# Order and shape of side work in a two-block transformer kernel on one TensorE: weights rounded ahead of the last evacuation, gate products with a 16-column stationary operand, squares and delta rule reordered

## The reference, cut to what matters

```
up = dwconv3(h @ w_in); gate, val = split(up)          # both MLPs, F = 5632
m  = (silu(gate) * val) @ w_out
x  = x + rmsnorm(m, norm_post_ffn)                     # first block: norm of the product
x  = x + m                                             # second block
gb, ga = the last 16 columns of h @ w_in_2             # 8 heads each
beta = sigmoid(gb)
g    = -exp(a_log) * softplus(ga + dt_bias);  g_cum = cumsum(g)  # per chunk of 64
q, k = l2norm(silu(conv4(q))) * 128 ** -0.5, l2norm(silu(conv4(k)))
lmat = where(strict, (k * beta) @ k.T * decay, 0);  t_inv = inv(eye + lmat)
attn = where(lower, q @ k.T * decay, 0)
out  = rmsnorm(delta_rule(q, k, v, beta, g), norm_g) * silu(z)
```

## Time and profile before

| | |
|---|---|
| median of three runs | 2841.45 us (2841.38 to 2842.84) |
| the profiled execution | 2843.84 us, its span 2842.0 us |
| mean granted TensorE clock | 0.989 |
| TensorE, its weight loads | 2770.0 us busy, 2390.9 us |
| VectorE, ScalarE, POOL | 1970.1, 1333.3 and 70.5 us busy |
| matmuls | 15280 |
| HBM read | 475.53 MB, 168 GB/s over the span |

### The profile page before, as it was taken

The page is one execution under the profiler, slowest core; times in us unless marked ns, Lnnn a source line. Parts: engine busy times, 40 slices in busy tenths (PEclk is TensorE's granted clock), DMA queues, the critical chain, the costliest instruction groups (busy, mean ns, idle before and its releaser), DMA issues.

```text
span 2842.0 us, 42751 instructions
## 1 busy us (share of the span) xinstructions
PE 2770.0 (97%) x15280; PEld 2390.9 (84%) x15280; DVE 1970.1 (69%) x2715; ACT 1333.3 (47%) x1651; POOL 70.5 (2%) x95
## 2 busy tenths in 40 slices
PE   7999999998999999999999999999999999999998
PEld 6888888887888888777788888887888888887886
DVE  5777777768888888644445676767578888885443
ACT  5444454436444444333455555566464444443443
POOL 0000000000000000000000000000000000000000
PEclk9999999999999999999989999999999999999999
DMA  6544444444555555555534533344445555555554
GB/s 209 167 159 156 161 155 153 156 154 141 185 196 179 193 191 186 176 188 183 181 112 164 170 128 117 123 152 159 160 160 195 178 194 189 185 198 179 184 186 140
DMA packets 131603, 479.28 MB, mean 169 GB/s; under 512 B 14688, under 2 KB 14864, under 8 KB 131360
## 3 DMA queue, kind: packets, MB, share of 16 engines
q1 hardware_dynamic: 130896, 474.15, 50.3%
q0 software_dynamic: 592, 3.53, 0.4%
HBM read 475.53 MB, written 2.10 MB: 168 GB/s over the span
## 4 chain that ended last, share of the span: by engine, by line
PE 91%; DVE 4%; ACT 3%; issue 1%; DMA 0%; DVEq 0%; ACTq 0%; SPq 0%
PE acc L391 37%; PE acc L393 19%; PE acc L414 7%; PE acc L416 7%; PE acc L415 7%; PE acc L367 4%; PE ps L1082 2%; PE acc L369 2%; DVE wts L318 1%; ACT wts L312 1%; PE ps L1587 1%; PE ps L1580 1%; PE ps L561 1%; ACT half L496 0%; ACT L524 0%
## 5 line engine op out<-in xcount | busy, mean ns | idle before, releaser
L391 PE MATMUL acc<-hs,wts 128*128 128x512 f32 x4672 | 1654.5, 397 | 9.6 <-DVE wts L318 5.0
L318 DVE TENSOR_TENSOR wts<-raw,wts 128x1024 fp32r<-128x1024 f32 x896 | 1065.5, 1224 | 575.1 <-ACT wts L312 575.0
L312 ACT ACTIVATE wts<-raw 128x1024 fp32r<-128x1024 f32 x896 | 925.9, 1055 | 934.7 <-PE acc L393 465.1
L393 PE MATMUL acc<-hs,wts 128*128 128x256 f32 x4672 | 1310.1, 280 | 0.0
L391 PEld LDWEIGHTS acc<-hs,wts 128*128 128x128 f32 x4672 | 882.3, 189 | 204.6 <-issue 11.0
L393 PEld LDWEIGHTS acc<-hs,wts 128*128 128x128 f32 x4672 | 882.4, 189 | 2.2 <-issue 2.2
L414 PE MATMUL acc<-wts,acts 128*128 128x512 f32 x704 | 278.7, 396 | 8.7 <-DVE wts L318 8.7
L416 PE MATMUL acc<-wts,acts 128*128 128x512 f32 x704 | 280.6, 399 | 0.0
L415 PE MATMUL acc<-wts,acts 128*128 128x512 f32 x704 | 277.6, 394 | 0.0
L326 ACT ACTIVATE half<-acc 128x512 f32<-128x512 f32 x162 | 96.9, 598 | 248.3 <-PE acc L393 229.8
L337 DVE TENSOR_TENSOR half<-acc,half 128x512 f32<-128x512 f32 x158 | 109.1, 691 | 100.9 <-ACT half L326 100.8
(11 more groups left out here) (298 smaller groups left out, 2249.6 us busy)
## 6 DMA issues: line engine op xcount, KB each, us to landing
raw<-stream SPq DMA_DIRECT2D x896, 512.0 KB, 3.7
xf<-xT SPq DMA_DIRECT2D x4, 512.0 KB, 8.2
memr<-memT POOLq DMA_DIRECT2D x1, 2048.0 KB, 9.1
outT<-memr SPq DMA_DIRECT2D x8, 256.0 KB, 2.4
KQ<-masks POOLq DMA_DIRECT2D x1, 448.0 KB, 5.6
vec<-vecs POOLq DMA_DIRECT2D x1, 352.0 KB, 5.9
cst<-consts POOLq DMA_DIRECT2D x1, 256.0 KB, 6.5
neg<-consts POOLq DMA_DIRECT2D x1, 192.0 KB, 2.6
```

The costliest lines, as they stand in the source:

```text
L312: nc.scalar.activation(whi[:, b, :], raw[:, b, :], ACT.Copy).then_inc(hi_ready, 1)
L318: nc.vector.tensor_tensor(wlo[:, b, :], raw[:, b, :], whi[:, b, :].bitcast(F32), ALU.subtract).then_inc(lo_ready, 1)
L391: nc.tensor.matmul(acc[:, 2 * par + n, :], whi[:, b, c:c + P], src[:, kt, :], start=start, stop=False)
L393: mm = nc.tensor.matmul(acc[:, 2 * par + n, 0:T], wlo[:, b, c:c + P], src[:, kt, 0:T], start=False, stop=stop)
```

## The change

- `wide_product` calls `end` for each half of a group. VectorE's order stays. ScalarE does the first half's squares ahead of the last block's rounding, and the second half's behind it; for down1 and for the last group of the held products both stand ahead.
- In the looped passes of both MLPs, ScalarE and VectorE take two blocks before the last evacuation of a pass, and none before the first block of the next; the down products skip the block that the last pass has taken for them.
- Gate products: the 16 weight columns are stationary and the tokens stream, 16 matmuls of 512 and 16 of 256 columns into 16 partitions, four pairs between half blocks. VectorE copies one half of the sum and adds the other, two transposes turn it to tokens by 16, and all that follows is as before, three calls earlier for the cumulative sums.
- Delta rule: VectorE multiplies k before q and TensorE does its four k k products before the four of q k; the Silu of z stands behind the two Exps; the table of Ln is loaded ahead after the squares of pair 0 and at the end of pairs 0 to 2.

```diff
@@ -455,37 +455,38 @@
                     if i == 1 and f and side is None:
                         drain(mid(f))
                     ahead = round_hi if what == "act" else take_lo
-                    if final and what == "dve":
-                        end(f, lap, k, grp)
+                    late = final and what == "act" and name != "down1" and not (held and f == 3)
+                    if final:
+                        end(f, lap, k, grp, 0)
+                        if not late:
+                            end(f, lap, k, grp, 1)
                     if held and final and f == 3:
-                        if what == "act":
-                            end(f, lap, k, grp)
                         continue
                     if i % 2 and side is not None:
                         next(side, None)
-                    if lap * SLOTS + k + AHEAD < N_BLOCKS:
+                    begun = k == 0 and name in ("down1", "down2")
+                    if lap * SLOTS + k + AHEAD < N_BLOCKS and not begun:
                         ahead(eng, lap, k + AHEAD)
                     if i % 2 == 0 and side is not None:
                         next(side, None)
-                    if final and what == "act":
-                        end(f, lap, k, grp)
+                    if late:
+                        end(f, lap, k, grp, 1)
...
@@ -498,15 +499,15 @@
 
         def square_sums(act, s, name, src):
 
-            def end(f, lap, k, grp):
-                for c in range(2):
-                    if c == 0:
-                        act.wait_ge(chunk_out, WIDE_AT[name] + grp + 1)
-                    else:
-                        act.wait_ge(evac, GROUP_AT[name] + grp + 3)
-                    ins = square(act, s, f, c, src[:, f, c])
-                ins.then_inc(NA[s].sem, 1)
-                if s == "n2" and f == 3:
+            def end(f, lap, k, grp, c):
+                if c == 0:
+                    act.wait_ge(chunk_out, WIDE_AT[name] + grp + 1)
+                else:
+                    act.wait_ge(evac, GROUP_AT[name] + grp + 3)
+                ins = square(act, s, f, c, src[:, f, c])
+                if c == 1:
+                    ins.then_inc(NA[s].sem, 1)
+                if c == 1 and s == "n2" and f == 3:
...
@@ -1179,13 +1176,15 @@
                 mid, end = keep_second(eng)
                 wide_product(eng, what, "hgout", os_, (3,), 1, mid, end, held=True)
 
+        joint = zm[0:16, 0, 0:T]
+
         def gate_scalar(act):
             act.wait_ge(gate_in, 32)
             nc.scalar.activation(tls[:, 0], tl[:], ACT.Copy).then_inc(gt_act.sem, 1)
             nc.scalar.activation(ea[:], gaw[:, 0:8], ACT.Exp).then_inc(gt_act.sem, 1)
             yield from pause(7)
             act.wait_ge(gt_vec.sem, gt_vec.count("a"))
-            lg = ps[:, 2, 0:32].rearrange("p (c n) -> p c n", c=2)
+            lg = ps[:, 3, 0:32].rearrange("p (c n) -> p c n", c=2)
             for c in range(2):
                 ins = nc.scalar.activation(gts[:, c, 0:8], lg[:, c, 0:8], ACT.Sigmoid, scale=factor("n5", c))
             ins.then_inc(gt_act.sem, 1)
@@ -1203,9 +1202,15 @@
         def gate_vector(dve):
             dve.wait_ge(gt_act.sem, gt_act.count("tlh"))
             nc.vector.tensor_tensor(tls[:, 1], tl[:], tls[:, 0].bitcast(F32), ALU.subtract).then_inc(gt_vec.sem, 1)
-            yield from pause(6)
+            yield from pause(5)
+            both = ps[0:16, 2, :].rearrange("p (s n) -> p s n", s=2)
+            dve.wait_ge(gt_pe.sem, gt_pe.count("both"))
+            nc.vector.tensor_copy(joint, both[:, 1]).then_inc(gt_vec.sem, 1)
+            dve.wait_ge(gt_vec.sem, gt_vec.count("half"))
+            nc.vector.tensor_tensor(joint, joint, both[:, 0], ALU.add).then_inc(gt_vec.sem, 1)
+            yield
             dve.wait_ge(gt_pe.sem, gt_pe.count("lg"))
-            lg = ps[:, 2, 0:32].rearrange("p (c n) -> p c n", c=2)
+            lg = ps[:, 3, 0:32].rearrange("p (c n) -> p c n", c=2)
             dve.wait_ge(NA["n5"].sem, NA["n5"].count("r"))
             for c in range(2):
                 ins = nc.vector.scalar_tensor_tensor(gt2[:, 0, c], lg[:, c, 8:16], factor("n5", c),
@@ -1232,17 +1237,20 @@
         def gate_tensor(pe):
             yield from pause(7)
             pe.wait_ge(gt_vec.sem, gt_vec.count("tll"))
+            for kt in range(DT):
+                if kt and kt % 4 == 0:
+                    yield
+                nc.tensor.matmul(ps[0:16, 2, :], tls[:, 0, kt, :], hs[:, kt, :], start=(kt == 0), stop=False)
+                mm = nc.tensor.matmul(ps[0:16, 2, 0:T], tls[:, 1, kt, :], hs[:, kt, 0:T], start=False,
+                                      stop=(kt == DT - 1))
+            mm.then_inc(gt_pe.sem, 1)
+            yield from pause(2)
+            pe.wait_ge(gt_vec.sem, gt_vec.count("sum"))
             for c in range(2):
-                yield from pause(2)
-                o = ps[:, 2, 16 * c:16 * c + 16]
-                for kt in range(DT):
-                    hi = hs[:, kt, c * P:(c + 1) * P]
-                    nc.tensor.matmul(o, hi, tls[:, 0, kt, :], start=(kt == 0), stop=False)
-                    nc.tensor.matmul(o, hi, tls[:, 1, kt, :], start=False, stop=False)
-                    mm = nc.tensor.matmul(o, hs[:, kt, T + c * P:T + (c + 1) * P], tls[:, 0, kt, :],
-                                          start=False, stop=(kt == DT - 1))
+                mm = nc.tensor.transpose(ps[:, 3, 16 * c:16 * c + 16], joint[:, c * P:(c + 1) * P],
+                                         ident[0:16, 0:16])
             mm.then_inc(gt_pe.sem, 1)
-            yield from pause(9)
+            yield from pause(6)
             pe.wait_ge(gt_vec.sem, gt_vec.count("g"))
             for c in range(2):
                 nc.tensor.matmul(ps[:, 1, 8 * c:8 * c + 8], row_le, gts[:, c, 8:16], start=True, stop=True)
@@ -1411,9 +1419,9 @@
             ins.then_inc(gd_vec.sem, 1)
             yield
             dve.wait_ge(gd_act.sem, gd_act.count("r", t))
+            nc.vector.tensor_tensor(gy[:, 1], gy[:, 1], gr[:, 2 * T:4 * T], ALU.mult).then_inc(gd_vec.sem, 1)
             nc.vector.scalar_tensor_tensor(gy[:, 0], gy[:, 0], float(P) ** -0.5, gr[:, 0:2 * T],
                                            ALU.mult, ALU.mult).then_inc(gd_vec.sem, 1)
-            nc.vector.tensor_tensor(gy[:, 1], gy[:, 1], gr[:, 2 * T:4 * T], ALU.mult).then_inc(gd_vec.sem, 1)
             nc.vector.tensor_copy(Tm[:], ident.unsqueeze(1).broadcast_to([P, 4, P])).then_inc(gd_vec.sem, 1)
             nc.vector.tensor_copy(TT[:], ident.unsqueeze(1).broadcast_to([P, 4, P])).then_inc(gd_vec.sem, 1)
             yield
@@ -1488,12 +1496,11 @@
             nc.scalar.activation(gy[:], gy[:], ACT.Silu).then_inc(gd_act_in.sem, 1)
             act.wait_ge(gd_act_in.sem, gd_act_in.count("silu", t))
             nc.scalar.activation(gs[:], gy[:, 0:2, :].rearrange("p a b -> p (a b)"), ACT.Square).then_inc(gd_act_in.sem, 1)
+            if t == 0:
+                nc.scalar.preload_act_table(ACT.Ln)
 
         def gd_scalar(act, t, par):
             flat = "p a b -> p (a b)"
-            act.wait_ge(evac, GROUP_AT["mix"] + 12 + 4 * t + 3 + 3)
-            nc.scalar.activation(gin[:, par, 3, :, 3:3 + T], gin[:, par, 3, :, 3:3 + T],
-                                 ACT.Silu).then_inc(gd_act.sem, 1)
             act.wait_ge(gd_pe.sem, gd_pe.count("ssq", t))
             nc.scalar.activation(gr[:].rearrange("p (a b) -> p a b", a=2), ps[:, 0:2, :], ACT.Ln,
                                  bias=EPS).then_inc(gd_act.sem, 1)
@@ -1504,7 +1511,11 @@
             act.wait_ge(gd_vec.sem, gd_vec.count("d", t))
             nc.scalar.activation(qd[:], rows[:, :, 1, :], ACT.Exp).then_inc(gd_act.sem, 1)
             nc.scalar.activation(DTr[:], DTr[:], ACT.Exp).then_inc(gd_act.sem, 1)
-            yield from pause(3)
+            yield
+            act.wait_ge(evac, GROUP_AT["mix"] + 12 + 4 * t + 3 + 3)
+            nc.scalar.activation(gin[:, par, 3, :, 3:3 + T], gin[:, par, 3, :, 3:3 + T],
+                                 ACT.Silu).then_inc(gd_act.sem, 1)
+            yield from pause(2)
             for lv in range(1, LEVELS):
                 act.wait_ge(gd_pe.sem, gd_pe.count(f"y{lv}", t))
                 nc.scalar.activation(half4(Z[:].rearrange(flat), lv, 0), half4(ps[:, 0, :], lv, 0),
@@ -1539,6 +1550,8 @@
             nc.scalar.activation(o_rms, ps[:, 1, :], ACT.Ln, bias=EPS, scale=1.0 / P).then_inc(gd_act_out.sem, 1)
             act.wait_ge(gd_act_out.sem, gd_act_out.count("oln", t))
             nc.scalar.activation(o_rms, o_rms, ACT.Exp, scale=-0.5).then_inc(gd_act_out.sem, 1)
+            if t < 3:
+                nc.scalar.preload_act_table(ACT.Ln)
             yield
 
         def gd_tensor(pe, t, par):
@@ -1559,6 +1572,8 @@
             pe.wait_ge(gd_vec.sem, gd_vec.count("k", t))
             for a in range(4):
                 nc.tensor.matmul(ps[:, 0, col(a)], gy[:, 1, col(a)], gy[:, 1, col(a)], start=True, stop=True)
```

(18 more changed lines are left out.)

67 lines of the change are left out of this document (31 added, 36 removed).

## The result

The changed kernel takes 2828.51 us (median of five, 2823.91 to 2830.58) against 2841.78 of the kernel before (five, 2841.38 to 2844.90): 13.3 us less, ratio 0.9949, interval [0.9938, 0.9960]. The forecast was 2817.5 with a range of 2810 to 2830. The direction held and the range did too, 1.5 us from its upper end; the size was 24 us and is 13.

The account below looks back on a forecast made before the run. TensorE, busy 97% of the span, was taken as the bound. Terms 10.35 + 4.5 + 2.7 + 2.3 - 1.3 - 0.2 - 1.1 + 6.7 = 23.9 us, from the median 2841.45, gave 2817.5 us, range 2810 to 2830.

Parts of the forecast that it names:

- the clock behind the new wait: Upper end of the range: half clock after the new wait before the cumulative sums, adding 3.3 us.
- the squares: Upper end of the range: reordered squares in the other wide products costing 6 us instead of 2.6, adding 3.4.
- the gate products at half clock: Upper end of the range: new gate matmuls taking 11.1 us instead of 5.5, adding 5.6.
- signs of being wrong: Any L391 waiting in the up-projection's passes, or a clock under 0.9 in the gates' stretch.
- Gate products: Gates' stretch: 18.75 us replaced by 5.5 plus 0.2, less a new 2.65 us wait before the sums; net 10.35.
- rival 1: Cold gates: narrow stationary operand or new wait lowers the clock, 1.7 to 8.5 us; time 2820 to 2826; chance 0.17.
- Starts of the down products: Block taken ahead removes TensorE's early waits: 4.5 us gained at the first down product, 2.7 at the second.
- Inside the loop: 42 looped MLP passes: next pass's first evacuation 0.05 to 0.1 us later, costing nothing.
- Rival 3: Looped passes start to wait, perhaps through late transfers; 24 to 46 us cost, up to 2864 us; chance 0.06.
- Order of the squares: Gains 2.3 us in the first down product; loses 1.3 at hgout, 0.2 in mixout, 1.1 in xo.
- Delta rule: Waits before its first product shrink and half clock behind one goes: 6.7 us gained, three Ln preloads counted.
- rival 2: More regained: preloads dropped or hidden (1.4, 1.4, 0.7 us) or sums in time (2.65); 2811 to 2815; chance 0.2.

Follow-up runs that it names:

- squares_old: Changed kernel with both squares of hgout, mixout, xo and down2 again behind the last block's rounding, down1 keeping both ahead: 2820.27 us.
- cum_late: Changed kernel with the sums over the tokens two calls later, at the 21st as in the kernel before: 2822.12 us.
- gates_alone: Kernel before with the new gate products alone, their sums over the tokens staying at the 21st call: 2830.60 us.
- best3: Changed kernel with the edits of cum_late, squares_old and ln_once together: 2811.98 us.
- silu_first: best3 with Silu of z moved back ahead of Ln and the preload of pair 0 dropped: 2821.04 us.
- ln_once: Changed kernel without the three preloads of Ln's table at the end of pairs 0 to 2: 2822.56 us.
- the control: The changed kernel run again unaltered, on the same chip as the first three follow-ups: 2826.40 us.

## Why the prediction was right or wrong

**The range: held, in part by luck.** Of the three terms that made its upper end, two came in full: the clock behind the new wait (3.3 us allowed, 3.4 measured) and the squares (6 allowed, 5.4 to 6.1 by squares_old). The third, the gate products at half clock (5.6), did not, and left room for losses that no bound held: 1.5 us in the first passes of the first MLP, 1.1 in mixout, 0.4 in the loops. Two of the prediction's own signs of being wrong came: the clock over the window of the earlier trace rows is 0.87, and an L391 waits in a looped pass (below).

**Gate products: right.** 18.75 us out and 5.7 in, 13.0 net; the stretch shows 12.9 in cum_late and 14.5 in gates_alone, 1.7 of it the half stretch at the opening. The wait of 2.65 us in front of the sums was forecast at the right place and measures 2.75 from start to start, 2.63 without the 0.12 that the matmul ahead of it takes. What failed was the half clock behind it, which the sum put at nothing: rival 1 had it at 1.7 to 3.3 us with a chance of 0.17, and it came in six of six traces with that wait. The net is 6.9 us instead of 10.35.

**Starts of the down products: right.** 4.5 and 2.7 us forecast. The second is 2.7. The first, with the group ends of down1, is 7.3 where 4.5 + 2.3 = 6.8 was forecast (the group ends alone are 2.6); the wait at the fifth block is 1.68 us, forecast 1.65, with the broadcast in front of it as worked out.

**Inside the loop: wrong.** "I find the first evacuation of the next pass 0.05 to 0.1 us later, and pay nothing for it." It is 0.5 later, and the first MLP pays 1.4 us here (1.2 to 2.5 in other executions); the second gains 1.0 (0.3 to 1.0). The step that failed is the 1.6 us by which the evacuations were to start later. It holds where the early block has landed in time (1.6 in best3's second MLP) and is 2.1 where ScalarE waits for its transfer, which in the first MLP is nearly every pass. Rival 3 had named this transfer, but the sum took none of it. The same cause stands behind 1.5 of the 2.8 us ahead of the loop (silu_first has 63.1 there and best3 61.6, with the same 6.8 us of half clock). In the first pass ScalarE waits for the early block 3.5 to 3.7 us in four of the eight traces (the changed kernel, cum_late, ln_once, silu_first) and 1.9 to 2.1 in the other four, the control among them; in the first four alone TensorE waits before the eighth block of the first looped pass. The changed kernel, then the control, then that wait:

```profile
697.58 1.06 ACT L312 ACTIVATE wts<-raw 128x1024 fp32r<-128x1024 f32 x1 [3.49 <-DMA raw<-stream]
```

```profile
696.41 1.06 ACT L312 ACTIVATE wts<-raw 128x1024 fp32r<-128x1024 f32 x1 [2.00 <-DMA raw<-stream]
```

```profile
715.85 0.50 PE L391 MATMUL acc<-hs,wts 128*128 128x512 f32 x1 [0.49 <-DVE wts L318]
```

This is read from the traces; why the transfer is later in some executions is open, and no run was made for it.

**Order of the squares: the sign right, the size short.** At hgout 1.3 us forecast, 1.5 measured, but half clock followed it into the next stage (1.3 us more). Mixout's 0.2 can't be told from nothing. In xo 1.1 us forecast, 2.3 measured: beside the group ends, the delayed last squares hold up the norm, and with it the opening of the second MLP, where TensorE waits 1 us at 2093. I had ended the replay at xo.

**Delta rule: right.** 6.7 forecast, 6.4 in the control (527.2 to 520.8), 5.4 in the first trace, which has the half stretch at 1924 besides. The waits before the products of k are under 1 us as said; of the three before the sums of squares, 0.8 us each, only the last pair's was foreseen. The preloads cost as worked out: 1.28 us each on ScalarE's chain, without the drain that the Trainium skill adds (ScalarE: Activation LUTs, What ACT_TABLE_LOAD costs); the next instruction stands right behind each load here as well (1699.05 and 1.28 is 1700.33, the weight block starts at 1700.34). The price of not having dropped them is 3.8 us, rival 2's case with 1.4, 1.4 and 0.7 us.

In sum, the forecast for the span was 2842.0 - 23.9 = 2818.1 us, 8.6 too low. The clock behind waits takes some 5.8 of it (3.4 at the gates, 1.3 at hgout, 1.1 at mixout), xo 1.2, the first passes of the first MLP 1.5, the two loops 0.4, the wait at hgout 0.2, and 0.5 came back at down1. Most of what I had left out was not a wait but what a wait brings: I counted the half clock that the change would remove, and none that it would bring.

## What to carry to other kernels

Price a new wait of TensorE with its clock: a wait of 2 to 3 us costs itself and often 1.7 to 3.4 us more where dense work follows, so an edit that trades a wait for nothing (the sums two calls early) should be moved until the wait is gone. A table loaded ahead serves only if no other table's function stands between it and its use; look at what is issued next on that engine, a turn later too. A block taken ahead needs its transfer ahead too: see in the trace whether it has landed. An edit inside a loop is worth what the one pass needs that has use for it: give it to that pass alone, and compare stretch by stretch between the same blocks, since the medians of two kernels 2 us apart don't tell them apart.
